# Paged sample attention: two page gathers asked for one block earlier, two rests of a weight made sooner, the last sequence in the order of the other seven

## The chip, the core and the metric

One core of one Trainium2 chip runs the whole program. The metric is the device time of one execution in microseconds (us), lower is better. Three timed runs of the kernel before are shown, and one execution was taken by the hardware profiler.

## The reference, cut to what matters

The program is one layer of a hybrid decoder for a prompt of 512 tokens and for 8 sample sequences of 4 new tokens each, with a past of 2048 tokens in pages. The part that the change touches is the sample's native sparse attention. For every sequence it compresses the past keys and values with a small network, scores the new queries against the compressed keys, selects blocks from these scores, and attends.

```python
past = cache_nsa_paged[l][page_table].reshape(b_s, past_len, 4, NSA_KV_HEADS, HEAD_DIM)
...
def compress_kv(k, pe, w1, w2):
    blocks = jnp.concatenate([kc[:, :-1], kc[:, 1:]], axis=2) + pe[None, None, :, None, :]
    flat = blocks.transpose(0, 1, 3, 2, 4).reshape(b, n_chunk - 1, g, CMP_BLOCK * d)
    return jax.nn.gelu(flat @ w1) @ w2
...
s = jnp.einsum('bqgrd,bcgd->bgrqc', qc, k_cmp) * scale
p_cmp, _ = masked_softmax(s, cmp_end[None, :] <= q_pos[:, None])
imp = jnp.einsum('bgrqc,cn->bgqn', p_cmp, cover)
top_val, top_idx = lax.top_k(score, SEL_TOPN)
```

The branch outputs then go through `w_branch_nsa` and `w_branch_dil`, the gates and `w_out`, and a mixture of experts follows.

## The kernel before, in words

The program is a chain of blocks. In a block each engine has its own written-out instruction stream, streams meet by semaphores, and all engines meet at the block's end. Three blocks matter here: `sample_dilated`, then `sample_nsa`, then `mix` (the products with the branch weights, the gates and `w_out`).

`sample_nsa` works in units of a (kind, sequence n, half h). The past of a sequence comes in two halves. `gather_half(pool, g)` with g = 2n + h is one indirect DMA on POOL's queue that brings half h of sequence n (2 MB, all four parts) into slot g % 3 of `sn_raw`. Gather 0 is asked for inside `sample_dilated`, gathers 1 and 2 are the first thing that POOL does in `sample_nsa`, and gather g from 3 on waits until slot g % 3 has been read. Slots 1 and 2 lie over buffers that `sample_dilated` still uses (`sd_kv` of kind g1), and slot 0 over none of them.

Units of kind k and v ("x units") take a half through these steps:
- `arrange` (DVE, L2351) reorders it into `sn_arranged`.
- `transposes` (PE, L2065) turns it into `sn_tp`.
- `copies` (ACT L2232, then DVE L119) writes it into `sn_xT` as an upper part and a rest. `sn_xT` holds two x units, so the copies of one wait for the products of the x unit two before it.
- `hidden` (PE, L125 to L127) multiplies it with the first compression weight, 24 products.

The weight too is held as an upper part (`cmp_w_upper`, ACT L2296) and a rest (`cmp_w_rest`, DVE L119, made by `rest_w1`), in four quarters. x unit number i of sequence 0 waits for quarter i.

Kind s turns the keys of the selected branch (PE L2052, copied by L2239 and L2369), and the s unit with h = 1 ends in `scores` (PE L2091). Kind p turns the probabilities of a pair of sequences (PE L2057) and waits for their exponentials on ACT (`exp_selected`, L2282). Kind c turns the small rest (L2059, L2061) and ends in `values` (L2129 to L2135). After sequence 3 there follow p and c of pair 0, after sequence 5 those of pair 1, after sequence 7 those of pair 2, and pair 3 closes. PE's loop turns unit u + 2 before it does the products of unit u.

At the end of sequence 7 PE does `compressed` (L2099, L2101), `scores_compressed` (L2106), two `products_ahead` with the dilated branch's weight (L2163 on `mx_w_dil`), and `importance` (L2119). `mx_w_dil` lies over `sn_xT`, so SP asks for it (L2582) only when the products of the last v unit are done:

```python
sp.wait_ge(s_mm, products_to(place["v", last, 1]))
self.load_branch(sp, "dil")
```

Of the kernel before, what the change touches and what calls it, by code (L numbers as in the profile page):

```python
# [12 lines left out]
TP, BS, SS = 512, 8, 4  # L13
# [72 lines left out]
RAW = 3  # L86
# [47 lines left out]
class Program:  # L134
# [1384 lines left out]
    def sample_dilated(self, oT):  # L1519
# [3 lines left out]
        k = self.k  # L1523
# [3 lines left out]
        with ExitStack() as s:  # L1527
# [56 lines left out]
            with self.nc.Block() as block:  # L1584
# [15 lines left out]
                @block.gpsimd  # L1600
                def _(pool):
                    pool.memset(self.qTz[:, 1], 0.0).then_inc(s_qz, 1)
                    pool.memset(pTz[:, :, :, :], 0.0).then_inc(s_zp, 1)
                    pool.wait_ge(s_tp, 8 * M)
                    pool.nop(nofuse=True)
                    self.gather_half(pool, 0)

                @block.tensor
                def _(pe):
# [260 lines left out]
    def sample_nsa(self, oT):  # L1870


        k = self.k
# [13 lines left out]

        for n in range(BS):
            order = [("k", 0), ("v", 0), ("s", 0), ("k", 1), ("v", 1), ("s", 1)]
            if n == BS - 1:  # L1890
                order = [("k", 0), ("v", 0), ("k", 1), ("v", 1), ("s", 0), ("s", 1)]
            for j, (kind, h) in enumerate(order):
                add(kind, n, h, j)
            if n % 2 == 1 and n > 1:
                add("p", n // 2 - 1, 0)
                add("c", n // 2 - 1, 0)
# [35 lines left out]
        def products_to(u):  # L1932
            return sum(kind in "kv" or (kind == "s" and h == 1) for kind, _, h, _ in units[:u + 1])
# [10 lines left out]
        with ExitStack() as s:  # L1944
# [55 lines left out]
            with self.nc.Block() as block:  # L2000
                @block.sync
                def _(sp):
                    last = BS - 1
                    g = 2 * last - 1
                    sp.wait_ge(s_tp, 2 * place["s", last - 1, 1] + 2)
                    sp.wait_ge(s_ar, x_units_to(place["v", last - 1, 1]) + 1)
                    sp.wait_ge(s_v, g + 1)
                    self.load_branch(sp, "nsa")
                    sp.wait_ge(s_mm, products_to(place["v", last, 1]))
                    self.load_branch(sp, "dil")  # L2010
                    sp.wait_ge(s_mm, products_to(place["s", last, 1]))
                    self.load_gates(sp, 0)

                @block.gpsimd
                def _(pool):
                    for g in range(1, RAW):
                        self.gather_half(pool, g)
                    for g in range(RAW, 2 * BS):
                        n, h = divmod(g - RAW, 2)
                        pool.wait_ge(s_tp, 2 * place["s", n, h] + 2)  # L2020
                        pool.nop(nofuse=True)
                        pool.wait_ge(s_ar, x_units_to(place["v", n, h]) + 1)
                        pool.nop(nofuse=True)
                        pool.wait_ge(s_v, g - RAW + 1)
                        pool.nop(nofuse=True)
                        self.gather_half(pool, g)

                @block.tensor
                def _(pe):
# [64 lines left out]
                    def compressed(n):  # L2094
                        misc_read_to("compressed", n)
                        pe.wait_ge(s_g, 2 * n + 2)
                        for g in range(KVH):
                            rows = slice(g * HD, (g + 1) * HD)
                            pe.matmul(mc[rows, 0:N1], self.w2k[:, g, rows], hid[:, 0, g, 0:N1], start=True, stop=True)  # L2099
                        for g in range(KVH):  # L2100
                            ins = pe.matmul(mc[0:N1, P + g * HD:P + (g + 1) * HD], hid[:, 1, g, 0:N1], self.w2v[:, :], start=True, stop=True)  # L2101
                        ins.then_inc(s_mw, 1)

                    def scores_compressed(n):
                        misc_read_to("scores_compressed", n)
                        pe.matmul(mc[half_row(n), 2 * P:2 * P + N1], self.qT_nsa[:, n // 4, 0, half_row(n)], kc[:, :],  # L2106
                                  start=True, stop=True).then_inc(s_mw, 1)
# [61 lines left out]
                    for u, (kind, n, h, j) in enumerate(units):  # L2169
                        if u + 2 < last_tail:  # L2170
                            transposes(u + 2)
                        if j == 0 and n > 0:
                            compressed(n - 1)
                        if j == 1 and n > 0:
                            scores_compressed(n - 1)
                        if n % 2 == 0:
                            if j == 2 and n >= 4:
                                turn_outputs(n // 2 - 2)
                            if j == 3 and n >= 2:
                                importance(n // 2 - 1)  # L2180
                            if j == 4:
                                scores_new(n // 2)
                        if j == 5 and n == BS - 1:
                            compressed(n)
                        if kind in "kvc" or (kind == "s" and h == 1):
                            pe.wait_ge(s_ed, u + 1)
                            pe.wait_ge(s_ea, 2 * u + 2)
                        if kind in "kv":
                            hidden(u)
                        elif kind == "s" and h == 1:  # L2190
                            scores(n)
                        elif kind == "c":
                            values(n)
                        if j == 5 and n == BS - 1:
                            scores_compressed(n)
                            products_ahead(0)
                            products_ahead(1)
                            importance(PAIRS - 1)
                        if u == last_tail - 1:
                            products_ahead(2)  # L2200
                            transposes(u + 1)
                            transposes(u + 2)
                            turn_outputs(PAIRS - 2)
                            products_ahead(3)
# [128 lines left out]
                def _(dve):  # L2333
# [170 lines left out]
                    for u, (kind, n, h, j) in enumerate(units[:last_tail]):  # L2504
                        if u + 1 < last_tail - 1:
                            copies(u + 1)
                        if u + 3 < last_tail:
                            arrange(u + 3)
                        if u < 2:
                            rest_w1(2 + u)  # L2510
                        if j == 0 and n > 0:
                            compressed_out(n - 1)
                        if j == 1 and n > 0:
                            scores_compressed_out(n - 1)
                        if n % 2 == 0:
                            if j == 1 and n >= 2:
                                max_compressed(n // 2 - 1)
                            if j == 2 and n >= 4:
                                outputs_out(n // 2 - 2)
                            if j == 2 and n >= 2:  # L2520
                                normalize_compressed(n // 2 - 1)
                            if j == 3 and n >= 2:
                                select_blocks(n // 2 - 1)
                            if j == 4:
                                scores_new_out(n // 2)
                            if j >= 4 and n >= 2:
                                mask_scores(n // 2 - 1, j - 4)
                        elif n >= 3 and 0 <= j < 2:
                            max_selected(n // 2 - 1, j)
                        if j == 5 and n == BS - 1:  # L2530
                            copies(u + 2)
                            compressed_out(n)
                        if kind == "s" and h == 1:
                            scores_out(n)
                        if j == 5 and n == BS - 1:
                            p = PAIRS - 1
                            scores_compressed_out(n)
                            max_compressed(p)
                            normalize_compressed(p)
                            max_of_blocks(p)  # L2540
                            select_blocks(p)
                            max_of_selected_blocks(p)
                            mask_scores(p, 0, s_nm)
                            mask_scores(p, 1, s_nm)
                        if kind == "c":
                            outputs(n)
# [1147 lines left out]
```

## Time and profile before

| what | us |
|---|---|
| median of the 3 timed runs | 1125.28 |
| lowest and highest of them | 1124.56, 1125.5 |
| time of the profiled execution | 1124.47 |
| its span (first to last instruction) | 1122.6 |
| PE busy, DVE busy, ACT busy, POOL busy in it | 1027.3, 478.7, 310.2, 148.2 |
| `sample_nsa` in it, from its first DVE instruction (519.03) to the first one of `mix` (741.70) | 222.7 |

The profile gives each instruction's start and duration in us from the span's start, and in brackets how long its engine had been idle before it and what ended that. PE's instructions overlap by some 0.16 us, so starts are the better clock: 24 products of an x unit start 0.12 us apart at the full granted clock. PEclk is the clock granted to TensorE, as a share of its full 2.4 GHz.

### The profile page before, as it was taken

To read this page: it belongs to the slowest core of one execution; us is meant where nothing else is said; L and a number is where in the kernel's file an instruction comes from. 1 tells how busy PE (TensorE), PEld (TensorE's weight loads), DVE (VectorE), ACT (ScalarE), POOL (GpSimd) and SP (SyncE) were. 2 spreads that over 40 slices of the span, in tenths; PEclk is the share of its full clock that TensorE was granted. 3 is DMA by queue.
4 is the path that set the end of the run, shared out by engine and by line. 5 is a ranking of instruction groups with operands and counts; after the bars stand their busy time and mean duration, and the time that the engine had idled before them with its cause. 6 is when DMAs were issued, how large, how long until landed. Compare 5 with 4: busy or idle time off the path is not lost. (4 is left out here: it accounts for less than half of the span.)

```text
span 1122.6 us, 20626 instructions
## 1 busy us (share of the span) xinstructions
PE 1027.3 (92%) x8408; PEld 770.3 (69%) x8408; DVE 478.7 (43%) x993; ACT 310.2 (28%) x678; POOL 148.2 (13%) x188
## 2 busy tenths in 40 slices
PE   6999999999889999897998989999998999789685
PEld 6999999899856667776987878775555433233232
DVE  6443324324257755544575857544226111010105
ACT  4100000211146643333565555501111111110103
POOL 0170000600015530000110000000001121110200
PEclk9999999999969999798999999999997999898999
DMA  8757861679364846686455434359726999999966
GB/s 260 244 221 297 300 239 42 174 254 354 95 221 150 298 146 198 196 276 242 175 202 226 150 152 150 119 188 337 310 75 252 379 424 423 424 424 425 423 258 251
DMA packets 100367, 279.92 MB, mean 249 GB/s; under 512 B 17764, under 2 KB 73984, under 8 KB 88896
## 3 DMA queue, kind: packets, MB, share of 16 engines
q1 hardware_dynamic: 90240, 229.57, 55.6%
q0 software_dynamic: 6976, 42.48, 9.9%
q10 hardware_dynamic: 3072, 6.75, 1.6%
q8 instruction: 57, 0.93, 0.3%
q14 instruction: 22, 0.18, 0.0%
HBM read 264.52 MB, written 69.53 MB: 298 GB/s over the span
## 5 line engine op out<-in xcount | busy, mean ns | idle before, releaser
L3134 PE MATMUL ex_up_ps<-ex_w_up,ex_hT 128*64 128x512 f32 x512 | 123.3, 637 | 27.1 <-DMA ex_w_up<-in_expert_w_up 25.9
L125 PE MATMUL proj_acc<-w_in_upper,hT_upper 128*128 128x328 f32 x352 | 112.3, 319 | 2.7 <-DVE hT_rest L119 2.3
L127 PE MATMUL proj_acc<-w_in_upper,hT_rest 128*128 128x328 f32 x352 | 110.5, 314 | 0.0
L3134 PEld LDWEIGHTS ex_up_ps<-ex_w_up,ex_hT 128*64 128x64 f32 x512 | 41.3, 146 | 97.7 <-issue 87.5
L126 PE MATMUL proj_acc<-w_in_rest,hT_upper 128*128 128x328 f32 x252 | 79.8, 317 | 0.0
L125 PE MATMUL sn_hp<-sn_xT,cmp_w_upper 128*128 128x256 f32 x256 | 76.6, 299 | 0.0
L125 PE MATMUL proj_acc<-hT_upper,merge_w_upper 128*128 128x272 f32 x256 | 74.3, 290 | 1.3 <-ACT qT_dil L564 1.3
L126 PE MATMUL proj_acc<-hT_rest,merge_w_upper 128*128 128x272 f32 x256 | 73.6, 288 | 0.0
L127 PE MATMUL proj_acc<-hT_upper,merge_w_rest 128*128 128x272 f32 x256 | 73.5, 287 | 0.0
L126 PE MATMUL sn_hp<-sn_xT,cmp_w_upper 128*128 128x256 f32 x256 | 73.2, 286 | 0.0
L127 PE MATMUL sn_hp<-sn_xT,cmp_w_rest 128*128 128x256 f32 x256 | 73.2, 286 | 0.0
L125 PEld LDWEIGHTS proj_acc<-w_in_upper,hT_upper 128*128 128x128 f32 x352 | 66.7, 189 | 4.5 <-DVE hT_rest L119 2.7
L3288 DVE TENSOR_TENSOR ex_act<-ex_silu,ex_up_ps 128x256 f32<-128x256 f32 x16 | 6.7, 421 | 144.7 <-ACT ex_silu L3224 144.7
L127 PEld LDWEIGHTS proj_acc<-w_in_upper,hT_rest 128*128 128x128 f32 x352 | 66.7, 190 | 0.0
L3157 PE MATMUL ex_down_ps<-ex_w_down,ex_actT 128*64 128x512 f32 x256 | 58.4, 597 | 1.3 <-ACT ex_actT L3234 1.3
L125 PEld LDWEIGHTS sn_hp<-sn_xT,cmp_w_upper 128*128 128x128 f32 x256 | 49.4, 193 | 2.2 <-issue 1.7
L126 PEld LDWEIGHTS sn_hp<-sn_xT,cmp_w_upper 128*128 128x128 f32 x256 | 49.5, 193 | 0.0
L127 PEld LDWEIGHTS sn_hp<-sn_xT,cmp_w_rest 128*128 128x128 f32 x256 | 49.4, 193 | 0.0
L125 PEld LDWEIGHTS proj_acc<-hT_upper,merge_w_upper 128*128 128x128 f32 x256 | 48.1, 188 | 1.7 <-ACT qT_dil L564 1.5
L127 PEld LDWEIGHTS proj_acc<-hT_upper,merge_w_rest 128*128 128x128 f32 x256 | 48.3, 189 | 0.0
L126 PEld LDWEIGHTS proj_acc<-hT_rest,merge_w_upper 128*128 128x128 f32 x256 | 48.1, 188 | 0.0
L126 PEld LDWEIGHTS proj_acc<-w_in_rest,hT_upper 128*128 128x128 f32 x252 | 48.0, 190 | 0.0
(537 smaller groups left out, 1962.7 us busy)
## 6 DMA issues: line engine op xcount, KB each, us to landing
ex_w_up<-in_expert_w_up SPq DMA_DIRECT2D x30, 2048.0 KB, 30.2
ex_w_down<-in_expert_w_down SPq DMA_DIRECT2D x32, 1024.0 KB, 34.8
out_dil_sample<-in_cache_dil_w SPq DMA_DIRECT2D x16, 1022.0 KB, 9.1
out_dil_sample<-in_cache_dil_w SPq DMA_DIRECT2D x4, 4088.0 KB, 15.8
w_in_chunk<-in_w_in SPq DMA_DIRECT2D x10, 1312.0 KB, 5.9
merge_w<-in_w_in SPq DMA_DIRECT2D x16, 512.0 KB, 6.5
sd_kv_g<-in_cache_dil_w SPq DMA_DIRECT2D x16, 512.0 KB, 6.8
rows<-in_cache_dil_w SPq DMA_DIRECT2D x16, 512.0 KB, 7.0
```

Source lines behind the costliest of these rows:

```text
L125: pe.matmul(out, a[0], b[0], start=first, stop=False)
L126: pe.matmul(out, a[0], b[1], start=False, stop=False)
L127: return pe.matmul(out, a[1], b[0], start=False, stop=last)
L3134: ins = pe.matmul(up_ps[r, q, :], hT[:, q, c, r], wu[slot][:, u, c, :], start=c == 0, stop=c == KD - 1)
L3157: ins = pe.matmul(dn_ps[r, half, :], aT[:, q, c, r], wd[slot][:, u, c, half * 512:(half + 1) * 512], start=c == 0, stop=c == 1)
L3288: dve.tensor_tensor(ac[:, q, :], sl[:, q, :], up_ps[:, q, FF:2 * FF], ALU.mult).then_inc(s_ac, 1)
```

## The change

Four edits.
1. Gathers 1 and 2 move from the head of POOL's stream in `sample_nsa` into `sample_dilated`, behind gather 0 and behind a wait until the last reader of the g1 buffers has run (the second count of `s_pv["g1"]`).
2. In DVE's loop `rest_w1(2)` and `rest_w1(3)` go ahead of `arrange(3)` and `arrange(4)`.
3. The last sequence loses its own order of units (k0 v0 k1 v1 s0 s1) and has that of the others (k0 v0 s0 k1 v1 s1).
4. With it `compressed(7)` follows `scores(7)` on PE, `compressed_out(7)` follows `scores_out(7)` on DVE, and SP waits for `compressed(7)` as well before it loads the gates over the buffer that this reads.

```diff
                     self.gather_half(pool, 0)
+                    pool.wait_ge(s_pv["g1"], 2)
+                    pool.nop(nofuse=True)
+                    for g in range(1, RAW):
+                        self.gather_half(pool, g)
...
             order = [("k", 0), ("v", 0), ("s", 0), ("k", 1), ("v", 1), ("s", 1)]
-            if n == BS - 1:
-                order = [("k", 0), ("v", 0), ("k", 1), ("v", 1), ("s", 0), ("s", 1)]
...
                     sp.wait_ge(s_mm, products_to(place["s", last, 1]))
+                    sp.wait_ge(s_mw, turn_no["compressed", last] + 1)
                     self.load_gates(sp, 0)
...
-                    for g in range(1, RAW):
-                        self.gather_half(pool, g)
                     for g in range(RAW, 2 * BS):
...
-                        if j == 5 and n == BS - 1:
-                            compressed(n)
...
                         if j == 5 and n == BS - 1:
+                            compressed(n)
                             scores_compressed(n)
                             products_ahead(0)
...
+                        if u < 2:
+                            rest_w1(2 + u)
                         if u + 3 < last_tail:
                             arrange(u + 3)
-                        if u < 2:
-                            rest_w1(2 + u)
...
                         if j == 5 and n == BS - 1:
                             copies(u + 2)
-                            compressed_out(n)
                         if kind == "s" and h == 1:
                             scores_out(n)
+                        if j == 5 and n == BS - 1:
+                            compressed_out(n)
```

DVE near the start of `sample_nsa`, from the copies of v0 of sequence 0 on. First before:

```order
L2351 COPY sn_arranged<-sn_raw_4924 128x1024
L119 TENSOR_TENSOR cmp_w1_rest_58<-cmp_w1,cmp_w1_upper 128x2x512
L2369 COPY sn_kT<-sn_tp0 128x512
L2351 COPY sn_arranged<-sn_raw_4924 128x1024
L119 TENSOR_TENSOR cmp_w1_rest_58<-cmp_w1,cmp_w1_upper 128x2x512
L119 TENSOR_TENSOR sn_xT<-sn_tp2,sn_xT 128x4x128
```

and the same place of the changed kernel:

```order
L119 TENSOR_TENSOR cmp_w1_rest_58<-cmp_w1,cmp_w1_upper 128x2x512
L2351 COPY sn_arranged<-sn_raw_4924 128x1024
L2369 COPY sn_kT<-sn_tp0 128x512
L119 TENSOR_TENSOR cmp_w1_rest_58<-cmp_w1,cmp_w1_upper 128x2x512
L2351 COPY sn_arranged<-sn_raw_4924 128x1024
L119 TENSOR_TENSOR sn_xT<-sn_tp2,sn_xT 128x4x128
```

Each of the two rests has changed places with the arrangement of a half next to it.

PE at the end of sequence 7, from the last product of unit v1 on. Before:

```order
L127 MATMUL sn_hp<-sn_xT,cmp_w_rest 128x256
L2057 MATMUL sn_tp<-ident,sn_scores 128x64 x16
L2059 MATMUL sn_tp<-ident,sn_scores_cmp 127x64
L2061 MATMUL sn_tp<-ident,sn_scores 32x64
L2099 MATMUL sn_misc<-sn_hidden,cmp_w_k 64x127 x2
L2101 MATMUL sn_misc<-cmp_w_v,sn_hidden 127x64 x2
L2091 MATMUL sn_ss<-sn_kT,sample_place 32x512 x4
L2106 MATMUL sn_misc<-sn_kc,sample_place 32x127
L2163 MATMUL sn_hp<-oT,mx_w_dil 128x256 x8
L2119 MATMUL sn_misc<-sn_scores_cmp,sample_place 64x127
```

and of the changed kernel, where every line number is one higher:

```order
L127 MATMUL sn_hp<-sn_xT,cmp_w_rest 128x256
L2060 MATMUL sn_tp<-ident,sn_scores_cmp 127x64
L2062 MATMUL sn_tp<-ident,sn_scores 32x64
L2092 MATMUL sn_ss<-sn_kT,sample_place 32x512 x4
L2100 MATMUL sn_misc<-sn_hidden,cmp_w_k 64x127 x2
L2102 MATMUL sn_misc<-cmp_w_v,sn_hidden 127x64 x2
L2107 MATMUL sn_misc<-sn_kc,sample_place 32x127
L2164 MATMUL sn_hp<-oT,mx_w_dil 128x256 x8
L2120 MATMUL sn_misc<-sn_scores_cmp,sample_place 64x127
```

The 16 turns of pair 2's probabilities (L2057) have left this place: they now stand before the 24 products of v1. The scores stand ahead of `compressed`.

DVE at the same end, from pair 2's probabilities on. Before:

```order
L2374 COPY sn_pT<-sn_tp 128x512
L2376 COPY sn_pT<-sn_tp 127x64
L2386 COPY sn_kc<-sn_misc 128x127
L2387 COPY sn_vc<-sn_misc 127x128
L2382 COPY sn_scores<-sn_ss 32x512 x2
L2391 COPY sn_scores_cmp<-sn_misc 32x127
```

and changed:

```order
L2374 COPY sn_pT<-sn_tp 128x512
L2376 COPY sn_pT<-sn_tp 127x64
L2382 COPY sn_scores<-sn_ss 32x512 x2
L2386 COPY sn_kc<-sn_misc 128x127
L2387 COPY sn_vc<-sn_misc 127x128
L2391 COPY sn_scores_cmp<-sn_misc 32x127
```

The two copies of the compressed keys and values now follow the two copies of the scores.

## Rows read from the trace of the kernel before

**Rows 1.** The page: span, and busy us (share) of each engine.
```profile
span 1122.6 us, 20626 instructions
PE 1027.3 (92%) x8408; PEld 770.3 (69%) x8408; DVE 478.7 (43%) x993; ACT 310.2 (28%) x678; POOL 148.2 (13%) x188
```

**Rows 2.** Timeline at the start of `sample_nsa`: start us, duration us, engine, line [idle before].
```profile
508.03 3.07 PE L1686 MATMUL sd_O<-sd_kv_g,sd_pTz 128*32 128x256 f32 x32 [0.77 <-DVE sd_pTz L1818]
...
519.99 1.17 POOL L1866 DMA_INDIRECT sn_raw<-in_cache_nsa_paged,page_rows  x1 [16.69 <-issue]
...
524.68 1.29 DVE L119 TENSOR_TENSOR sn_xT<-sn_tp,sn_xT 128x512 fp32r<-128x512 f32 x2
...
528.07 0.28 PE L127 MATMUL sn_hp<-sn_xT,cmp_w_rest 128*128 128x256 f32 x1
529.50 0.69 DVE L2351 COPY sn_arranged<-sn_raw 128x1024 f32<-128x1024 f32 x1 [3.52 <-DMA sn_raw<-in_cache_nsa_paged,page_rows]
530.10 1.22 DVE L119 TENSOR_TENSOR cmp_w_rest<-cmp_w,cmp_w_upper 128x1024 fp32r<-128x1024 f32 x1
530.34 0.85 PE L2065 MATMUL sn_tp<-ident,sn_arranged 128*128 128x128 f32 x6 [1.98 <-DVE sn_arranged L2351]
```

**Rows 3.** The tile `sn_raw`: its 16 gathers from issue to landing.
```profile
DMA to landing us min/median/max: 7.9/8.9/13.0
```

**Rows 4.** Timeline of PE in sequence 3: v0, pair 0's turns, v1, scores.
```profile
591.02 0.39 PE L125 MATMUL sn_hp<-sn_xT,cmp_w_upper 128*128 128x256 f32 x1
...
600.32 1.18 PE L2057 MATMUL sn_tp<-ident,sn_scores 64*128 64x64 f32 x16 [1.51 <-ACT sn_scores L2282]
601.43 0.39 PE L125 MATMUL sn_hp<-sn_xT,cmp_w_upper 128*128 128x256 f32 x1
...
604.83 1.07 PE L2091 MATMUL sn_ss<-sn_kT,sample_place 128*32 128x512 f32 x8
```

**Rows 5.** Timeline of PE in sequence 5: pair 1's turns, and the scores after v1.
```profile
649.86 1.18 PE L2057 MATMUL sn_tp<-ident,sn_scores 64*128 64x64 f32 x16 [1.50 <-ACT sn_scores L2282]
...
655.86 1.06 PE L2091 MATMUL sn_ss<-sn_kT,sample_place 128*32 128x512 f32 x8
```

**Rows 6.** Timeline of PE, DVE and SP's queue at the end of sequence 7.
```profile
685.88 1.07 PE L2065 MATMUL sn_tp<-ident,sn_arranged 128*128 128x128 f32 x8 [0.32 <-DVE sn_arranged L2351]
...
691.98 0.39 PE L125 MATMUL sn_hp<-sn_xT,cmp_w_upper 128*128 128x256 f32 x1
...
699.53 0.37 PE L125 MATMUL sn_hp<-sn_xT,cmp_w_upper 128*128 128x256 f32 x1
...
702.70 0.39 SPq L2582 DMA_DIRECT2D mx_w_dil<-in_w_branch_dil  x1
702.99 1.18 PE L2057 MATMUL sn_tp<-ident,sn_scores 64*128 64x64 f32 x16 [0.32 <-ACT sn_scores L2282]
...
705.24 0.44 PE L2099 MATMUL sn_misc<-sn_hidden,cmp_w_k 128*64 128x127 f32 x4 [0.91 <-ACT sn_hidden L2252]
...
707.79 1.40 DVE L2382 COPY sn_scores<-sn_ss 32x512 f32<-32x512 f32 x2 [1.00 <-PE sn_ss L2091]
708.10 4.67 PE L2163 MATMUL sn_hp<-oT,mx_w_dil 128*128 128x256 f32 x16
...
712.70 0.43 PE L2119 MATMUL sn_misc<-sn_scores_cmp,sample_place 64*64 64x127 f32 x2
713.38 0.29 DVE L2417 COPY sn_imp<-sn_misc 64x127 f32<-64x127 f32 x1
```

**Rows 7.** The tile `mx_w_dil`: from issue to landing.
```profile
DMA to landing us min/median/max: 5.1/5.1/5.1
```

**Rows 8.** Stretches: length, busy us (instructions) of each engine, PEclk, DMA share, GB/s.
```profile
600.30:604.60 4.30, 4.28 (x41) 4.09 (x42) 1.29 (x2) 2.58 (x4) 0.00 (x0) 1.00 0.96 408
...
652.00:655.40 3.40, 3.40 (x18) 3.36 (x16) 0.00 (x0) 0.59 (x2) 0.00 (x0) 0.50 0.60 255
...
706.70:710.00 3.30, 3.30 (x15) 1.86 (x8) 2.17 (x6) 2.57 (x5) 0.00 (x0) 0.50 0.39 79
```

## The prediction

> **What bounds the kernel now.** I read the page first: PE is busy for 1027.3 of 1122.6 us, the other engines for less than half [rows 1]. So a wait counts only where PE stands still. I then asked for PE's waits inside `sample_nsa` and for the timeline around each place that the diff touches. The reader is to see four things.
>
> At the start, PE starts the last product of the first unit (k0) at 528.07 and then idles 1.98 us. DVE had stood still for 3.52 us until gather 1 landed and then arranged half 1 at 529.50. That gather was asked for at 519.99 [rows 2].
>
> In the regular order (sequence 3) PE idles 1.51 us before pair 0's turns at 600.32, because ACT's exponentials are late. Sequence 5 has the same wait, 1.50 us [rows 4, 5]. In sequence 7, whose order is its own, this wait is only 0.32 us, since 24 products more lie ahead of it [rows 6].
>
> At the end of sequence 7, SP asks for `mx_w_dil` at 702.70, as soon as v1's products are done. It lands 5.1 us later, at 707.80 [rows 7], and the first product with it starts at 708.10, so it is just in time. PE fills these 5.4 us with pair 2's turns, `compressed` and the scores [rows 6].
>
> The granted clock is 1.00 right after the wait in sequence 3, and 0.50 (the lower of the two levels, 1.2 GHz) from 652.0 on after the same wait in sequence 5, and again from 706.7 on after the 0.32 and 0.91 us waits [rows 6, 8].
>
> **The change part by part.** Times are on the axis of the profile before.
>
> *Gathers 1 and 2.* The g1 values' last reader starts at 508.03 and takes 3.07 us, so POOL is released at about 511.1, 8.9 us ahead of 519.99. Behind POOL's new wait stand only these two issues (1.17 us for the one seen) and the block's end, which comes at 519.03 at the earliest; nobody waits for POOL there. With the slowest landing, 13.0 us [rows 3], gather 1 is there by 524.1 and gather 2, issued 1.2 us behind, by 525.3. DVE needs them from 525.97 on (524.68 + 1.29) [rows 2].
>
> *Rests sooner.* DVE now does a rest of 1.22 us and then the arrangement of 0.69 us: 525.97 + 1.22 + 0.69 = 527.9. PE is free at 528.2, so the rest is hidden behind the products of the first unit with 0.3 us to spare; were that cover gone, it would cost up to 1.22. The edit is worth nothing by itself. The second rest lies beside v0's products likewise. What is late next is nothing up to sequence 1: DVE's and ACT's copies come as early as PE's turns. Term: -2.0 (from 1.98; start to start it would be 530.34 - 528.19 = 2.15).
>
> *Start of sequence 7.* In the old order unit k1 is turned two places after v0, and waits for the last gather: 0.32 us at 685.88 [rows 6]. In the new order s0 stands there, whose half is long in place. Term: -0.3.
>
> *End of sequence 7.* I lay sequence 3's distances onto sequence 7, from the first product of v0 (591.02 there, 691.98 here). Pair 2's turns then start at +9.30, 701.28, after a wait of 1.5 us. v1's products start at +10.41, 702.39, where they started at 699.53. They end, as SP sees it, 3.17 us later (702.70 - 699.53), at 705.56. `mx_w_dil` then lands at 710.66. The first product with it started at 708.10, so it moves by 2.56. The scores start at +13.81, 705.79. DVE copies them first (1.40 us) and the compressed keys after, which would let `scores_compressed` go at about 708.9 and the products ahead at 709.3. That is earlier than 710.66, so edit 4's order is hidden behind the transfer; were the transfer early, it would cost 709.3 - 708.1 = 1.2. The two products ahead take 4.60 us (708.10 to 712.70), partly at clock 0.50. I keep that, since PE will have idled still more just before. `importance` and DVE's copy of it (713.38) follow with the same shift. Behind this PE, DVE and ACT run as before. Term: +2.6.
>
> *Gates.* SP's load waits for `compressed(7)`, at about 707.7. Nothing stands behind it but the next block's loads. Even at 13.0 us, the longest landing seen here, it is there 20 us before `mix` starts at 741.7. Term: 0.
>
> The loads of `mix` and the experts are issued after `sample_nsa`, so the shift carries to the end. Sum: -2.0 - 0.3 + 2.6 = +0.3. The profiled execution would go from 1124.47 to 1124.8. It lies 0.8 under the median of the runs, so the forecast is 1125.28 + 0.3 = 1125.6.
>
> The bounds of the unknown costs: v1 at the lower clock. Turns to scores took 4.51 us in sequence 3 (604.83 - 600.32) and 6.00 in sequence 5 (655.86 - 649.86) [rows 4, 5], so 0 to +1.5. The products ahead at full clock: of the 3.3 us at 0.50 [rows 8], 1.9 lie in them, so 0 to -0.95. The stretch at 652.0 may go as PE's waits shift by 2 us, or another may come: -1.5 to +1.5.
>
> For the landing I took the row's 5.1 us. The Trainium skill ("DMA: Bandwidth & Descriptors", Anatomy of one DMA) fits about 2.0 us plus the bytes at 436 GB/s, for GpSimd's path; for this 1 MB that is an estimate of 4.4 us, 0.7 less than the row, and the sum by it would be -0.4.
>
> **The rivals.**
>
> *A, forecast: the two ends cancel.* Two us gained at the head, 2.6 lost because v1's end, and with it the transfer, comes 2.9 us later. +0.3, with -1.9 to +2.2 around it.
>
> *B, slower: the new 1.5 us wait lowers the clock.* Place: pair 2's turns, then v1's 24 products at 0.50, which also delays the transfer. For it: sequence 5; against it: sequence 3 with the same wait and 1.00. Price +1.5, so +1.8, 1127.1. It passes the border only with a second such stretch, in the values behind `importance` or in sequence 3: 1.7 more (half of 3.4 us at 0.50, rows 8) gives +3.5, 1128.8. The Trainium skill ("TensorE: Matmul & The Clock Gate", HAM oscillation) says that waits between bursts of matmuls send the clock to half and the next burst starts slow. [...] The trace bears it out in one of these two cases.
>
> *C, faster.* The waits shift such that the stretch at 652.0 and the one in the products ahead vanish: 0.3 - 1.5 - 0.95 = -2.2, with the 2.15 instead of 2.0 at the head -2.3: 1123.0.
>
> *D: the gathers do not come early, or the block's end waits for them.* Gather 0 was asked for 17 us ahead of that end, so no row excludes a wait. Gather 2 landing at 521 (8.9 us, the median) to 525.3 would move 519.03 by 2 to 6.3, on top of A's +0.3: +2.3 to +6.6, say 1130. If they simply come no sooner, the 2.0 are missing: +2.3.
>
> **How the numbers follow.** Chances: A 0.63, B with one stretch 0.12, with two 0.09, C 0.12, D 0.04. The measurement tells 0.2%, 2.25 us, from no change. Faster (under 1123.0): C for the most part and the edge of A, 0.14. Slower (over 1127.5): B with two, D, half of B with one, the edge of A, 0.22. Same: 0.64. The range 1123.0 to 1128.2 takes in C and B with one stretch, leaves out D and the far end of B, some 0.15.
>
> **What the profile after would show.** Right: gathers 1 and 2 issued near 511; no idle time before PE's turns near 528; the order rest, arrangement on DVE; 1.5 us of idle before L2058 in sequence 7; an idle time of 1 to 2 us before L2164 at `mx_w_dil`, with the DMA as releaser or none named; `sample_nsa` 222.7 us long again within 2. Wrong: L2164 starting within 0.5 us of `scores_compressed`; `exp_selected` done before PE asks for it; gather 1 landing after 527. More or fewer stretches at clock 0.50 between 519 and 741 than before would move the time by 1.5 to 1.7 each, and are what would most easily make the number wrong.

## The result: about 6 us slower, and the profile after

| | before | after |
|---|---|---|
| median of 11 timed runs each, us | 1125.28 | 1131.65 |
| lowest and highest, us | 1121.27, 1128.89 | 1129.63, 1133.25 |
| profiled execution, us | 1124.47 | 1131.37 |
| its span, us | 1122.6 | 1129.4 |

The ratio is 1.0053, with a 95% interval of 1.0038 to 1.0069: the changed kernel is slower, by some 6 us (4.3 to 7.8). The forecast was 1125.6 and its range ended at 1128.2, so the time lies outside it. The page of the changed kernel begins:

```profile
span 1129.4 us, 20627 instructions
PE 1024.5 (91%) x8408; PEld 765.4 (68%) x8408; DVE 478.5 (42%) x993; ACT 311.2 (28%) x678; POOL 148.5 (13%) x188
```

PE does the same 8408 matmuls in 2.8 us less than in [rows 1], and the span is 6.8 us longer. So PE stands still for longer. Where it does so is seen in the timeline at the seam of the two blocks:

```profile
511.51 2.61 PE L1690 MATMUL sd_O<-rows,sd_pTz 128*32 128x256 f32 x32
512.58 0.95 POOL L1870 DMA_INDIRECT sn_raw<-in_cache_nsa_paged,page_rows  x1 [9.32 <-PE sd_O L1690]
513.84 0.94 POOL L1870 DMA_INDIRECT sn_raw<-in_cache_nsa_paged,page_rows  x1 [0.30 <-issue]
...
519.26 0.19 DVE L1837 COPY oT<-sd_tq 128x32 f32<-128x32 f32 x1 [0.71 <-PE sd_tq L1713]
526.17 1.05 ACT L2296 CAST cmp_w_upper<-cmp_w 128x1024 fp32r<-128x1024 f32 x1 [18.15 <-PEq L1584]
526.20 1.29 DVE L2351 COPY sn_arranged<-sn_raw 128x1024 f32<-128x1024 f32 x2 [6.75 <-PEq L1584]
526.95 3.31 PE L2066 MATMUL sn_tp<-ident,sn_arranged 128*128 128x128 f32 x15 [7.72 <-DVE sn_arranged L2351]
```

The same place in the kernel before:

```profile
518.52 0.19 DVE L1833 COPY oT<-sd_tq 128x32 f32<-128x32 f32 x1 [0.71 <-PE sd_tq L1709]
519.03 1.30 DVE L2351 COPY sn_arranged<-sn_raw 128x1024 f32<-128x1024 f32 x2 [0.32 <-PEq L1584]
519.78 3.68 PE L2065 MATMUL sn_tp<-ident,sn_arranged 128*128 128x128 f32 x16 [1.30 <-DVE sn_arranged L2351]
521.46 0.94 POOL L1866 DMA_INDIRECT sn_raw<-in_cache_nsa_paged,page_rows  x1 [0.30 <-issue]
```

Gathers 1 and 2 are asked for at 512.58 and 513.84 instead of 519.99 [rows 2] and 521.46. The dilated block's last work ends at 519.45, and then nothing runs on any compute engine until 526.17. The row of `sn_arranged` calls this an idle time of 6.75 us ended by PE's sequencer at L1584, the line at which the dilated block is opened and closed. The half that is arranged at 526.20 is the one of gather 0, which was asked for 24 us before. The DMA engines show what is going on meanwhile. Columns of this view of stretches: length, busy us (instructions) of PE, PEld, DVE, ACT and POOL, PEclk, DMA share, GB/s:

```profile
519.50:522.00 2.50, 0.00 (x0) 0.00 (x0) 0.00 (x0) 0.00 (x0) 0.00 (x0) 0.54 1.00 426
522.00:524.00 2.00, 0.00 (x0) 0.00 (x0) 0.00 (x0) 0.00 (x0) 0.00 (x0) 0.50 1.05 451
524.00:524.50 0.50, 0.00 (x0) 0.00 (x0) 0.00 (x0) 0.00 (x0) 0.00 (x0) 0.50 0.76 328
524.50:525.00 0.50, 0.00 (x0) 0.00 (x0) 0.00 (x0) 0.00 (x0) 0.00 (x0) 0.50 0.09 33
525.00:526.10 1.10, 0.00 (x0) 0.00 (x0) 0.00 (x0) 0.00 (x0) 0.00 (x0) 0.50 0.00 0
```

All engines stand idle while the gathers stream in, and for 1.1 us more in which the DMA engines move nothing. The tile view of `sn_raw`, cut to the two early issues, gives the landings: 8.3 us after issue for gather 1 and 11.9 us for gather 2, the highest of the row.

```profile
DMA to landing us min/median/max: 8.3/10.1/11.9
```

Gather 2 has thus landed at 513.84 + 11.9 = 525.7, and 0.4 us later the next block starts. POOL's own rows end after 0.95 us and show nothing of this. The Trainium skill ("Perfetto Trace Analysis", DMA Instruction, SWDGE) says that such a row ends when the descriptors are made and not when the data has moved, and the trace agrees: 0.94 us in the row, 11.9 us to the landing.

The start of sequence 0 after that, the rows that answer to [rows 2]:

```profile
533.05 1.22 DVE L119 TENSOR_TENSOR cmp_w_rest<-cmp_w,cmp_w_upper 128x1024 fp32r<-128x1024 f32 x1
534.18 0.69 DVE L2351 COPY sn_arranged<-sn_raw 128x1024 f32<-128x1024 f32 x1
...
535.01 1.06 PE L2066 MATMUL sn_tp<-ident,sn_arranged 128*128 128x128 f32 x8 [0.71 <-DVE sn_arranged L2351]
```

DVE does not wait for a gather any more, and the rest stands ahead of the arrangement.

The end of sequence 7, the rows that answer to [rows 6]:

```profile
696.27 0.39 PE L125 MATMUL sn_hp<-sn_xT,cmp_w_upper 128*128 128x256 f32 x1
...
705.58 1.18 PE L2058 MATMUL sn_tp<-ident,sn_scores 64*128 64x64 f32 x16 [1.51 <-ACT sn_scores L2282]
706.68 0.39 PE L125 MATMUL sn_hp<-sn_xT,cmp_w_upper 128*128 128x256 f32 x1
...
711.34 0.38 SPq L2583 DMA_DIRECT2D mx_w_dil<-in_w_branch_dil  x1
...
711.55 1.07 PE L2092 MATMUL sn_ss<-sn_kT,sample_place 128*32 128x512 f32 x8
...
714.65 0.40 PE L2107 MATMUL sn_misc<-sn_kc,sample_place 128*32 128x127 f32 x2 [1.09 <-DVE sn_vc L2387]
...
716.43 3.69 PE L2164 MATMUL sn_hp<-oT,mx_w_dil 128*128 128x256 f32 x16 [1.37 <-DMA mx_w_dil<-in_w_branch_dil]
```

The 1.51 us wait before pair 2's turns, the late request for `mx_w_dil`, its landing and PE's wait for it of 1.37 us are all there. `mx_w_dil` takes 5.0 us to land, against 5.1 in [rows 7]. Between the turns and the scores, the stretch 707.30 to 710.90 has a granted clock of 0.53:

```profile
707.30:710.90 3.60, 3.60 (x20) 3.60 (x19) 0.00 (x0) 0.87 (x2) 0.00 (x0) 0.53 0.00 0
```

That is almost wholly the lower level, 1.2 GHz, and it falls on v1's 24 products.

Behind them, PE's values (L2130) wait for DVE's copy of the importance (L2417):

```profile
719.04 0.18 DVE L2446 TENSOR_REDUCE sn_block_max<-sn_scores 64x1 f32<-64x32 f32 x1
720.05 0.43 PE L2120 MATMUL sn_misc<-sn_scores_cmp,sample_place 64*64 64x127 f32 x2
720.58 0.29 DVE L2417 COPY sn_imp<-sn_misc 64x127 f32<-64x127 f32 x1 [1.36 <-PE sn_misc L2120]
```

This copy starts 4.15 us after the first product with `mx_w_dil` (720.58 - 716.43), where before it started 5.28 us after it (713.38 - 708.10) [rows 6]. There DVE's reduction stood right ahead of the copy:

```profile
713.16 0.18 DVE L2446 TENSOR_REDUCE sn_block_max<-sn_scores 64x1 f32<-64x32 f32 x1
714.03 1.96 PE L2129 MATMUL sn_misc<-sn_v,sn_pT 128*32 128x128 f32 x64 [0.90 <-DVE sn_imp L2417]
```

With PE's starts as marks, the whole difference of the two profiled executions can be laid out:

| piece | before | after | difference |
|---|---|---|---|
| up to the dilated block's last copy | 518.71 | 519.45 | +0.74 |
| from there to the first arrangement | 0.32 | 6.75 | +6.43 |
| to the scores of sequence 0 (543.93; 548.60) | 24.90 | 22.40 | -2.50 |
| to the scores of sequence 6 (684.50; 689.15) | 140.57 | 140.55 | -0.02 |
| to v0's first product in sequence 7 | 7.48 | 7.12 | -0.36 |
| to the first product with `mx_w_dil` | 16.12 | 20.16 | +4.04 |
| to `mix` (741.70; 748.89) | 33.60 | 32.46 | -1.14 |
| from `mix` to the end | 380.90 | 380.51 | -0.39 |

The sum is +6.8, the difference of the spans. The seam gives +6.43 - 2.50 = +3.9, and the last sequence -0.36 + 4.04 - 1.14 = +2.5. `sample_nsa` itself, from its first DVE instruction on, takes 222.69 us (748.89 - 526.20) and took 222.67: as forecast, what it gains at its head it loses at its end. The whole loss stands ahead of its first instruction.

### The profile page after: what moved, and what is told of

Its sections match the earlier page's. It is cut to its first block and busy times, and to the rows that moved or that the text cites. A ratio compares the mean times of both kernels' runs of the same rounds, so it can differ in the third digit from the quotient of the medians.

```text
span 1129.4 us, 20627 instructions
## 1 busy us (share of the span) xinstructions
PE 1024.5 (91%) x8408; PEld 765.4 (68%) x8408; DVE 478.5 (42%) x993; ACT 311.2 (28%) x678; POOL 148.5 (13%) x188
## 3 DMA queue, kind: packets, MB, share of 16 engines
q10 hardware_dynamic: 3072, 6.75, 1.6%
```

## The experiments

Each ratio below is against the kernel before timed beside that run. The median of these runs ranged from 1124.97 to 1128.06 us, so 0.001 is about 1.1 us, and times in us of different experiments are not compared.

**Theory 1**: a block's end includes a wait until POOL's own transfers, the indirect gathers, have landed. In the kernel before, gather 0 was asked for 17 us ahead of the end, so nothing showed. **Rivals**: gathers 1 and 2 slow the block's last work or the weight's copies by their traffic; POOL's new wait holds the block whatever is in flight; or the loss is the last sequence's order.

The block has an option that leaves this wait of POOL out of its end. It doesn't touch the semaphores by which `arrange` waits for its gather. It is the tool for the first experiment, which is the changed kernel with this line in `sample_dilated`:

```diff
-            with self.nc.Block() as block:
+            with self.nc.Block(no_gpsimd_drain=True) as block:
```

> The changed kernel, with the end of the dilated block built so that GpSimd does not wait for its own DMA queue there; nothing else differs. Theory 1 (the block's end waits until the gathers have landed): the first arrangement of half 0 starts within 0.5 us of the last copy of the block instead of 6.9 us behind it, PE's long idle time there goes from 7.7 to about 1.3 us, and the time falls by 6 to 7 us against the changed kernel, to about the level of before (0 to +2 us). Theory 2 (the early gathers hold up the start in another way: their traffic, or the start of the next block's code): the gap stays within 1 us of 6.9 and the time stays 5 to 7 us over before.

Measured: ratio 0.9997 of before (0.9972 to 1.0023), where the changed kernel has 1.0053: 6.3 us less, as theory 1 expected. The span is 1122.4. The same place in its timeline:

```profile
513.23 0.95 POOL L1870 DMA_INDIRECT sn_raw<-in_cache_nsa_paged,page_rows  x1 [9.06 <-PE sd_O L1690]
514.48 0.94 POOL L1870 DMA_INDIRECT sn_raw<-in_cache_nsa_paged,page_rows  x1 [0.30 <-issue]
519.68 0.19 DVE L1837 COPY oT<-sd_tq 128x32 f32<-128x32 f32 x1 [0.71 <-PE sd_tq L1713]
520.62 1.30 DVE L2351 COPY sn_arranged<-sn_raw 128x1024 f32<-128x1024 f32 x2 [0.75 <-PEq L1584]
```

The gathers go out at the same point of the program, the last copy starts 0.4 us later than in the changed kernel, and the gap is 0.75 instead of 6.75 us (theory 1 had it within 0.5, so it is a little longer than expected). Nothing but the wait has been taken away. So it is the block's end that waits, and neither the traffic nor POOL's wait for the readers.

**The gathers alone**: the kernel before with edit 1 only.

```diff
                     self.gather_half(pool, 0)
+                    pool.wait_ge(s_pv["g1"], 2)
+                    pool.nop(nofuse=True)
+                    for g in range(1, RAW):
+                        self.gather_half(pool, g)
```

> The kernel before with edit 1 alone (gathers 1 and 2 asked for in the dilated block), old order of the last sequence, rests as before. Theory 1: the gap at the block's end is there in full (about 7 us), the wait of 1.98 us near 528 is gone, so +4.5 to +5.5 us over before. Theory 2 (most of the loss comes from the last sequence's order): less than +2.5 us over before.

Measured: ratio 1.0027 (1.0002 to 1.0051), which is +3.0 us (0.2 to 5.8). That is less than the +4.5 to +5.5 of theory 1, though the interval reaches there, and this time alone would not exclude theory 2. The trace decides. Its gap is 7.27:

```profile
512.30 0.94 POOL L1870 DMA_INDIRECT sn_raw<-in_cache_nsa_paged,page_rows  x1 [0.30 <-issue]
517.32 0.19 DVE L1837 COPY oT<-sd_tq 128x32 f32<-128x32 f32 x1 [0.71 <-PE sd_tq L1713]
524.78 1.30 DVE L2353 COPY sn_arranged<-sn_raw 128x1024 f32<-128x1024 f32 x2 [7.28 <-PEq L1584]
```

The next block again starts 12.5 us after the last issue (524.78 - 512.30; in the changed kernel 526.20 - 513.84 = 12.4), though the dilated block was done 1.9 us sooner. The scores of sequence 0 start 29.7 us behind the dilated block's last copy, against 25.2 before, which is the +4.5 that was expected. The start follows the gathers and not the work.

**All but the gathers**: the changed kernel with gathers 1 and 2 back at the head of `sample_nsa`.

> The changed kernel without edit 1: gathers 1 and 2 again at the head of the paged block, with edits 2 to 4. Theory 1: no gap at the block's end, the wait near 528 is back (2 us, or up to 1.2 longer since a rest of the weight now stands ahead of it only if the gather is early, so unchanged), and the last sequence costs what the prediction gave it: +2.0 to +3.0 us over before. Theory 2: +5 us or more over before.

Measured: ratio 1.0016 (0.999 to 1.0042), gap 0.32, as in the kernel before. The gap is gone with edit 1. The time is +1.8 us (-1.1 to +4.7), just under the expected +2.0 to +3.0 and not told from none. The last sequence is dearer than before here too (61.3 us against 57.2 in the table below), in a trace with one stretch at half clock more.

**The gathers and the rests without the wait**: the kernel before with edits 1 and 2 and the option of the first experiment, the last sequence in its old order.

> The kernel before with edits 1 and 2 and the dilated block's end without GpSimd's wait for its DMA queue; the last sequence in its old order. Theory 1: the two us of the early gathers are kept and nothing is paid: -1.5 to -2.5 us against before, the fastest of the four. Theory 2: slower than before by 4 us or more.

Measured: ratio 0.9975 (0.9947 to 1.0003), the lowest of the four, gap 0.75, scores of sequence 0 at 23.1 us behind the dilated block's end, against 25.2 before. That is -2.8 us, a little past the expected -1.5 to -2.5, and the interval just reaches 1.

**The dose: one gather instead of two.** If the end waits for a landing, it must move with the size in flight.

```diff
                     self.gather_half(pool, 0)
+                    pool.wait_ge(s_pv["g1"], 2)
+                    pool.nop(nofuse=True)
+                    self.gather_half(pool, 1)
...
-                    for g in range(1, RAW):
-                        self.gather_half(pool, g)
+                    self.gather_half(pool, 2)
```

> The kernel before with gather 1 alone asked for early, gather 2 at its old place, the dilated block's end unchanged. Theory 1 (the block's end waits until the gathers on POOL's queue have landed): one gather of 2 MB asked for near 511.0 lands in 8 to 9 us instead of the 12.5 that the pair took, so the gap between the dilated block's last DVE work and the first arrangement is 1.5 to 3 us, not 0.3 and not 7. The time is then near that of before: +1.2 to +2.7 at the block's end, -2.0 at PE's wait for half 1. Rival (POOL's wait for the readers of the g1 buffers, or the issue itself, holds the block, whatever the size in flight): a gap of about 7 as with two.

Measured, in one profiled execution: gap 2.63.

```profile
510.58 0.95 POOL L1869 DMA_INDIRECT sn_raw<-in_cache_nsa_paged,page_rows  x1 [8.51 <-PE sd_O L1689]
519.69 1.36 DVE L2353 COPY sn_arranged<-sn_raw 128x1024 f32<-128x1024 f32 x2 [2.63 <-PEq L1584]
520.33 0.94 POOL L1869 DMA_INDIRECT sn_raw<-in_cache_nsa_paged,page_rows  x1 [8.79 <-POOLq L1584]
```

Its first arrangement starts at 519.69, 9.1 us after the issue. The gather landed 8.4 us after it, at 519.0. One gather gives 9.1 us, two give 12.4 to 12.5.

**Gather 0 asked for late.** This puts the kernel before's own gather into the place where it must hurt.

```diff
+                    pool.wait_ge(s_pv["g1"], 2)
+                    pool.nop(nofuse=True)
                     self.gather_half(pool, 0)
```

> The kernel before with gather 0 alone moved behind the wait for the g1 values' second reader, so that it is asked for near 511 instead of 502; gathers 1 and 2 stay at the head of the next block. Theory 1: gather 0 lands 8 to 9 us later, near 519.5 to 520, so that the gap at the block's end is 1 to 2.5 us where before had 0.32; the next two gathers and PE's wait for half 1 move with it, and the profiled time grows by about the gap. Rival (what holds the block in the changed kernel is that gathers 1 and 2 overlap with its last loads): a gap of 0.3, since gather 0 is asked for in both kernels.

Measured, in one profiled execution: issue at 512.71, first arrangement at 521.89, 9.2 us later, gap 2.72.

```profile
512.71 1.18 POOL L1868 DMA_INDIRECT sn_raw<-in_cache_nsa_paged,page_rows  x1 [55.49 <-PE sd_O L1688]
521.89 1.36 DVE L2353 COPY sn_arranged<-sn_raw 128x1024 f32<-128x1024 f32 x2 [2.73 <-PEq L1584]
```

That is 0.2 above the expected 1 to 2.5, since the issue came later than the 511 that was assumed. The rival's 0.3 is ruled out. Here `arrange` needs the same gather, so this run alone could not tell the block's end from the arrangement's own wait; the one before it can, since half 1 is not needed at that point.

**Edit 2 tested**: the kernel before with edit 1 and the option, without edit 2.

> The kernel before with gathers 1 and 2 early and the dilated block's end without the wait for POOL's queue; the rests and the last sequence stay as before. Theory 1: the gap is 0.7 to 0.8 us, PE's wait of 1.98 for half 1 is gone, and DVE arranges half 1 ahead of the rest. Against the same kernel with the rests made sooner (measured at 0.9975 of before) the difference is under 1 us: the rest is hidden behind the first unit's products, so 0.9970 to 0.9995 of before. Rival (the rests' order is worth something): over 1.5 us slower than with the rests sooner, with a wait for the third or fourth quarter of the rest in PE.

Measured: ratio 0.9978 (0.9953 to 1.0002), against 0.9975 with edit 2. The scores of sequence 0 start 23.1 us behind the dilated block's end in both. Edit 2 is worth nothing here, within what these times can tell.

**Edits 3 and 4 alone**:

> The kernel before with edits 3 and 4 alone, the last sequence in the order of the others; gathers and rests as before. From the prediction's own terms, -0.3 + 2.6: sample_nsa 2.3 us longer, 225.0, with a wait of 1.5 us before pair 2's turns and one of 1.0 to 1.5 at mx_w_dil; ratio 1.000 to 1.004. Theory 2 (the order costs nothing, all of the loss is the block's end): length within 0.5 of 222.7. Theory 3 (the order costs more, from the clock): 4 us or more longer, with more stretches at clock 0.50 between 680 and 720.

Measured: ratio 1.0025 (1.0013 to 1.0037). `sample_nsa` is 228.16 us long, +5.5, in a run with one stretch at 0.50 more at either end of it. The head is not edit 3's doing: PE's wait there is 3.22 instead of 1.98 us, though the gather landed in the same 9.5 us. PE had come to its end of the first unit sooner, and its turns then ran at half clock:

```profile
529.00 0.69 DVE L2349 COPY sn_arranged<-sn_raw 128x1024 f32<-128x1024 f32 x1 [3.54 <-DMA sn_raw<-in_cache_nsa_paged,page_rows]
...
529.85 1.94 PE L2064 MATMUL sn_tp<-ident,sn_arranged 128*128 128x128 f32 x8 [3.22 <-DVE sn_arranged L2349]
...
701.72 1.18 PE L2056 MATMUL sn_tp<-ident,sn_scores 64*128 64x64 f32 x16 [1.51 <-ACT sn_scores L2280]
...
712.53 5.38 PE L2162 MATMUL sn_hp<-oT,mx_w_dil 128*128 128x256 f32 x16 [1.29 <-DMA mx_w_dil<-in_w_branch_dil]
```

Both waits that the prediction set for the last sequence are there (1.51 and 1.29). The length as a whole fits theory 3 by its number, and which part of it is the order is read from the table of all kernels below. The ratio fits the 1.000 to 1.004 of the prediction's own terms, and its interval excludes that the order costs nothing.

**A control, the wait taken out of the kernel before**:

> The kernel before, with the dilated block's end freed of the wait for POOL's queue and nothing else changed. Theory 1 (the wait ends when the gathers in flight have landed): gather 0, asked for near 502, has landed before the block ends near 518.7, so there is nothing to gain: gap 0.3 to 0.8 us, first scores 25 to 26 us behind the dilated block's last DVE work, ratio 0.998 to 1.002. Rival (the wait itself costs time whatever is in flight): a gap under 0.2 and a ratio of 0.997 or less.

Measured: ratio 0.9979 (0.996 to 0.9998), gap 0.74, scores of sequence 0 at 24.2. The gap fits, the ratio is 0.0001 below what theory 1 allowed, and the scores are 0.8 us too early for it. Gather 1 was asked for 1.03 us behind the dilated block's last copy instead of 1.28, and landed in 8.8 us instead of 9.5:

```profile
518.40 1.30 DVE L2351 COPY sn_arranged<-sn_raw 128x1024 f32<-128x1024 f32 x2 [0.75 <-PEq L1584]
518.69 1.24 POOL L1866 DMA_INDIRECT sn_raw<-in_cache_nsa_paged,page_rows  x1 [15.40 <-POOLq L1584]
...
527.46 0.69 DVE L2351 COPY sn_arranged<-sn_raw 128x1024 f32<-128x1024 f32 x1 [2.12 <-DMA sn_raw<-in_cache_nsa_paged,page_rows]
```

So POOL starts about 0.25 us sooner without the wait even where nothing is in flight, by one trace of each. Whether the faster landing has to do with it is not known.

This trace also shows the old order's end of sequence 7 without any half clock:

```profile
709.73 0.43 PE L2119 MATMUL sn_misc<-sn_scores_cmp,sample_place 64*64 64x127 f32 x2
711.01 0.18 DVE L2446 TENSOR_REDUCE sn_block_max<-sn_scores 64x1 f32<-64x32 f32 x1
711.23 0.29 DVE L2417 COPY sn_imp<-sn_misc 64x127 f32<-64x127 f32 x1
711.87 1.96 PE L2129 MATMUL sn_misc<-sn_v,sn_pT 128*32 128x128 f32 x64 [1.72 <-DVE sn_imp L2417]
```

`importance` starts 3.62 us after the first product with `mx_w_dil` (706.11), 1.0 us sooner than before (4.60). But DVE is busy with its reductions and copies it only at 711.23, 5.12 us after that product against 5.28 before, and PE waits 1.72 us instead of 0.90. So in the old order it is DVE that sets the pace here, and the half clock in the products ahead cost next to nothing.

**The fastest once more**, on the chip of the control:

> The fastest version so far once more, on the chip of the control: the kernel before with gathers 1 and 2 early and without the wait at the dilated block's end. If its -2 us at the head is real, the ratio is again 0.996 to 0.999, and the scores of sequence 0 start 23.1 us behind the dilated block's last DVE work, against 25.2 before. If the first measurement was chance, the ratio is 1.000 or more.

Measured: ratio 0.9987 (0.9966 to 1.0009), scores of sequence 0 at 22.7.

All kernels beside each other. The first number is from the dilated block's last copy to the scores of sequence 0, the next two are the lengths of the following parts of `sample_nsa`, each with its number of stretches at granted clock 0.50, which last 3.4 us each:

| kernel | to scores of 0 | scores 0 to 6 (stretches) | scores of 6 to `mix` (stretches) | ratio |
|---|---|---|---|---|
| before | 25.2 | 140.6 (1) | 57.2 (1) | 1 |
| changed | 29.1 | 140.6 (1) | 59.7 (1) | 1.0053 |
| changed, no wait at the end | 23.2 | 140.5 (1) | 58.3 (0) | 0.9997 |
| edit 1 | 29.7 | 139.1 (0) | 58.8 (2) | 1.0027 |
| edits 2, 3, 4 | 26.4 | 140.5 (1) | 61.3 (2) | 1.0016 |
| edits 1, 2, no wait | 23.1 | 142.1 (2) | 59.3 (2) | 0.9975 |
| gather 1 early | 25.4 | 140.5 (1) | 59.5 (2) | one run |
| gather 0 late | 27.1 | 142.0 (2) | 59.4 (2) | one run |
| edit 1, no wait | 23.1 | 139.1 (0) | 58.9 (2) | 0.9978 |
| the same again | 22.7 | 142.1 (2) | 59.1 (2) | 0.9987 |
| no wait | 24.2 | 140.5 (1) | 57.2 (0) | 0.9979 |
| edits 3, 4 | 26.5 | 140.6 (1) | 61.4 (2) | 1.0025 |

The middle column is 139.1 us plus 1.45 for each stretch, whatever was edited. In the last column the new order is dearer at every number of stretches: 58.3 against 57.2 with none, 59.7 against 57.2 with one, 61.3 to 61.4 against 58.8 to 59.5 with two. So the order costs 1.1 to 2.6 us, by where the stretches fall. In the old order the first stretch cost nothing (57.2 with none and with one).

## Why the prediction was wrong

**The step that failed** is the one in the term for gathers 1 and 2 that reads "Behind POOL's new wait stand only these two issues (1.17 us for the one seen) and the block's end, which comes at 519.03 at the earliest; nobody waits for POOL there". The kernel's description says that all engines meet at the block's end, so everybody waits for POOL there, and POOL waits for its gathers to land. The term was set at -2.0 and is +6.43 - 2.50 = +3.9. That the end waits for the landing is shown: the start of the next block follows the last issue by 9.1 and 9.2 us with one gather in flight and by 12.4 and 12.5 with two, and with the wait left out the gap is 0.75. With that wait out, the head comes to what was predicted: 25.2 to 23.1 or 23.2 in three kernels, -2.0 to -2.1. Not all of it is the early gathers' work, since the control without them has 24.2.

This was rival D. Its mechanism and its price (2 to 6.3 at the seam, +2.3 to +6.6 in all, against +6.43 and about +6.4 measured) fit, at the upper end, only its chance of 0.04 did not. The prediction had seen that no row excluded the wait, since gather 0 had been asked for 17 us ahead, and still gave it the least chance. A wait that no row excludes, at a place that every engine passes, deserved far more; the range would then have had to reach to the end of its price, 1125.28 + 6.6 = 1131.9.

**Gathers, landing**: the issues came at 512.58 and 513.84, about 1.5 us later than the 511.1 and 512.3 of the working (0.7 of that is the later end of the whole block here), and gather 2 landed at 525.7. Without the block's end in the way that would have been early enough.

**Rests**: worth nothing, as forecast, and in the changed kernel at a price. The cover of 0.3 us was as thin as stated. In the changed kernel the granted clock had spent its low stretch in the idle seam, so PE was through with the first unit sooner, and the rest ahead of the arrangement was bare by 0.71 us (the wait at 535.01). Turn to turn PE took 535.01 - 526.95 = 8.06 us instead of 530.34 - 519.78 = 10.56, which is the -2.50: 1.27 of it is less waiting, and the other 1.23 is the clock.

**Start of sequence 7**: -0.3 forecast, -0.36 measured.

**End of sequence 7**: +2.6 forecast, +4.04 - 1.14 = +2.9 measured. The size is near, in part by luck. The distances of sequence 3 held: from v0 to the turns +9.31 (9.30 forecast), to v1 +10.41 (10.41). v1 then ran at half clock, 1.5 us longer, which was the upper end of the bound 0 to +1.5, and delayed the request for `mx_w_dil`. Against it stands the -1.14, and here a step of the prediction was wrong: "`importance` and DVE's copy of it (713.38) follow with the same shift". The products ahead ran at full clock, 3.69 instead of 4.67 us, and DVE was ahead of them: it copied the compressed scores (L2391) at 715.10, 1.33 us before the first product, where before it did so at 709.22, 1.12 us behind it. Its reductions were thus done at 719.22, before `importance` at 720.05, and its copy of the importance came 1.13 us sooner behind the first product. How much of that lead is PE's wait for `mx_w_dil` and how much edit 4's order on DVE is not separated. Full clock alone is not enough: in the old order at full clock (the control) the copy waits for DVE, and from the first product with `mx_w_dil` to `mix` it is 33.44 us, against 33.60 before and 32.46 or 32.47 in the changed kernel with and without the wait. The bound of -0.95 for full clock in these products was thus worth next to nothing in the old order and was paid out only in the new one. Without any such stretch, in the changed kernel with no wait at the block's end, the first product with `mx_w_dil` comes 25.8 us after the scores of sequence 6, against 23.6 before: +2.2, where -0.3 + 2.56 was worked out. With the 1.0 us that comes back behind it, the order costs 1.1 us where no stretch falls on it. Edit 4's order was hidden behind the transfer as said, with PE waiting 1.37 us for `mx_w_dil` in the end.

**Gates**: nothing waits for them, as forecast.

**Rival B**, the half clock after the 1.5 us wait: the trace shows the stretch behind pair 2's turns in three of the four kernels with the new order, and not in the fourth. The twelve traces hold 28 such waits of 1.5 us before turns of probabilities (sequences 3 and 5 in each, sequence 7 in the four). Behind 16 of them the granted clock fell to 0.50, 0.7 to 2.2 us after the turns began, and behind 12 it stayed at 1.00; between the scores of sequences 0 and 6 it fell nowhere else. But seven of the eight kernels with the old order have a stretch at the end of sequence 7 too, from 2.2 to 3.7 us behind the start of pair 2's turns, where PE's waits are 0.32 and 0.91 us. So the new wait did not bring a stretch where there was none. Between before and changed it lies on other work: before on the products ahead, where it cost next to nothing, and then on v1's products, where it cost 1.5 us. Whether the 1.5 us wait is what moved it is not shown. The Trainium skill ("TensorE: Matmul & The Clock Gate", HAM oscillation) says that a wait for a transfer that outlasts the burst of matmuls before it brings the clock down, so that the next burst starts slow. The waits here are much shorter than the work before them, so that is not this case. By these rows a fall behind such a wait is about as likely as none.

**The sum**: with the measured term at the seam in place of -2.0, the prediction's own other terms give +3.9 - 0.3 + 2.6 = +6.2, 1131.5, and 1131.65 was measured. That it fits so closely is luck in part: 1.23 of the -2.50 is the clock, and the +0.74 ahead of the seam and the -0.39 behind `mix` are in no term.

**What stays open**: whether the early gathers are worth anything in the whole time once the end doesn't wait. The four kernels without the wait in the old order have 0.9975, 0.9978, 0.9979 and 0.9987, one of them without early gathers, and their intervals overlap. In the traces the early gathers bring the scores of sequence 0 forward by 1.1 to 1.6 us against the one without (24.2), which is below what these times can tell apart. For the same reason it is open how much of the 1.5 to 2.8 us by which the four stand below before comes from the wait left out and how much from the gathers.

## What to carry to other kernels

A transfer on POOL's queue is cheap to ask for early only if the block in which it is asked for ends after it has landed: add the landing time (8 to 13 us for 2 MB here) to the issue and compare it with the block's end before counting any gain. Where a wait cannot be seen because it was always long over, that is no evidence against it. And a difference of some 2 us in a kernel with stretches of half clock is read from stage lengths sorted by the number of such stretches, not from the totals.

## What the runs showed that was not expected

- The end of a block waits for POOL's indirect transfers: the seam was 6.75 and 7.27 us with two gathers in flight, 2.63 with one, 0.32 with none and 0.74 to 0.75 with the wait left out. With the wait left out the seam is thus 0.4 us longer than with the wait and nothing in flight; why is not known.
- The stretches of granted clock 0.50 (1.2 GHz) last about 3.4 us, and up to 13.7 us at the seam. One costs some 1.45 us in the middle of `sample_nsa` (139.1, 140.5 and 142.0 with none, one and two of them). One that falls where PE is idle or waits for another engine anyway costs little or nothing: in the changed kernel the clock is at 0.50 from 519.7 to 526.9, in which no matmul ran, and in the old order's products ahead it cost 0.04 us (57.20 against 57.16 for the last part).
- Of the 4.0 us by which PE came later to `mx_w_dil`, 1.1 us came back behind it, since DVE was no longer late with the importance.
